# Expert blocks and first norm: bounds read at two loop ends, one 4 MB weight transfer per expert, another order of experts, and no barrier behind the first norm

## The reference, cut to what matters

```
h  = rms_norm(x, g)  * (1 + scale)  + shift        # 1024 tokens
hc = rms_norm(xc, g) * (1 + cscale) + cshift       # 256 tokens
u  = h @ w_in ; uc = hc @ w_in                     # gated convolution, attention, ...
```

```
hid = silu(x_block @ w_gate[e]) * (x_block @ w_up[e])      # 512 wide
y   = hid @ w_down[e]                                      # 1024 wide
out[token] += weight * y[row of the token]                 # two rows for each token
```

## Time and profile before

| what | us |
|---|---|
| median of three runs | 4255.51 |
| the profiled execution | 4245.79 |
| its span | 4243.7 |
| PE busy, in the span | 3750.0 |
| DVE busy | 1724.6 |
| ACT busy | 975.1 |
| expert stage of the first layer, first matmul to last store started | 2473 to 3031 |
| expert stage of the second layer, likewise | 3613 to 4164 |

### The profile page before, as it was taken

The page is one execution under the profiler, slowest core; times in us unless marked ns, Lnnn a source line. Parts: engine busy times, 40 slices in busy tenths (PEclk is TensorE's granted clock), DMA queues, the critical chain, the costliest instruction groups (busy, mean ns, idle before and its releaser), DMA issues.

```text
span 4243.7 us, 81332 instructions
## 1 busy us (share of the span) xinstructions
PE 3750.0 (88%) x29964; PEld 2095.4 (49%) x29965; DVE 1724.6 (41%) x3835; ACT 975.1 (23%) x2286; POOL 272.6 (6%) x453
## 2 busy tenths in 40 slices
PE   5997888999999889999988969989499998899874
PEld 3564665555444555444565445555344444455443
DVE  2585666413202664152465334434331114343335
ACT  3003545302001332131053212222120002222211
POOL 0000000000000000000000021111100000211111
PEclk9998999999999999999999989999799998999997
DMA  8111222101101000110142178999511113799994
GB/s 314 44 40 40 100 88 113 70 24 40 59 20 40 1 1 11 50 48 31 60 160 102 75 283 354 425 426 425 221 40 40 40 61 120 318 366 418 426 426 150
DMA packets 94333, 644.11 MB, mean 152 GB/s; under 512 B 18640, under 2 KB 41240, under 8 KB 60752
## 3 DMA queue, kind: packets, MB, share of 16 engines
q10 hardware_dynamic: 28896, 386.28, 21.5%
q1 hardware_dynamic: 46928, 194.98, 12.4%
q0 software_dynamic: 18336, 60.44, 4.1%
HBM read 594.70 MB, written 46.92 MB: 151 GB/s over the span
## 4 chain that ended last, share of the span: by engine, by line
PE 37%; DMA 13%; DVE 4%; issue 3%; SPq 2%; ACT 1%; DVEq 1%; ACTq 1%; POOLq 0%; POOL 0%
PE banks L258 23%; DMA y_tok<-arena 7%; PE banks L2407 7%; DMA arena<-in_w_gu 4%; SPq L2360 2%; PE banks L2416 2%; DMA arena<-y_tok,arena 1%; PE banks L1519 1%; DVE arena L1634 1%; PE banks L2122 1%; PE banks L2402 1%; PE banks L467 1%; DMA h_tok<-arena 0%; PE banks L2398 0%; ACTq L2300 0%
## 5 line engine op out<-in xcount | busy, mean ns | idle before, releaser
L258 PE MATMUL banks<-arena 128*128 128x512 f32 (+2 forms) x4544 | 1750.0, 547 | 39.0 <-ACTq L137 16.9
L258 PEld LDWEIGHTS banks<-arena 128*128 128x128 f32 x4544 | 841.4, 191 | 935.6 <-issue 884.6
L2407 PE MATMUL banks<-arena 128*32 128x256 f32 x10240 | 611.1, 387 | 48.2 <-DMA arena<-in_w_gu 41.1
L2407 PEld LDWEIGHTS banks<-arena 128*32 128x32 f32 x10240 | 324.4, 111 | 278.9 <-issue 104.8
L2416 PE MATMUL banks<-arena 128*32 128x256 f32 x5120 | 302.5, 384 | 65.4 <-DVE arena L2561 40.9
L2416 PEld LDWEIGHTS banks<-arena 128*32 128x32 f32 x5120 | 167.8, 110 | 194.0 <-DVE arena L2561 94.3
L1588 PE MATMUL banks<-arena 128*64 128x128 f32 x1952 | 161.8, 285 | 54.9 <-ACT arena L1601 39.2
L945 DVE SCALAR_TENSOR_TENSOR arena<-arena 128x1024 f32<-128x1024 f32 x240 | 195.9, 879 | 0.2 <-DVEq L137 0.2
L301 DVE SCALAR_TENSOR_TENSOR arena<-banks,arena 128x512 f32<-128x512 f32 (+1 forms) x72 | 51.9, 721 | 333.3 <-PE banks L258 333.3
L2373 POOL DMA_INDIRECT arena<-h_tok,arena x176 | 172.1, 978 | 142.2 <-POOL arena L2370 141.4
L1519 PE MATMUL banks<-arena 64*128 64x256 f32 (+2 forms) x768 | 130.1, 470 | 37.7 <-ACT arena L1690 32.8
(11 more groups left out here) (327 smaller groups left out, 3500.8 us busy)
## 6 DMA issues: line engine op xcount, KB each, us to landing
arena<-in_w_gu ACTq DMA_DIRECT2D x120, 2048.0 KB, 16.6
arena<-in_w_dn ACTq DMA_DIRECT2D x60, 2048.0 KB, 17.2
arena<-in_w_ada SPq DMA_DIRECT2D x24, 2048.0 KB, 7.3
y_tok<-arena SPq DMA_DIRECT2D x648, 32.0 KB
arena<-in_w_gu SPq DMA_DIRECT2D x8, 2048.0 KB, 10.8
y_tok<-arena POOLq DMA_DIRECT2D x1, 12800.0 KB, 36.3
arena<-in_ab_w_ada SPq DMA_DIRECT2D x6, 2048.0 KB, 9.5
arena<-in_cd_w_ada SPq DMA_DIRECT2D x6, 2048.0 KB, 7.3
```

The costliest lines, as they stand in the source:

```text
L258: last = pe.matmul(self.bank_of(g, n), lhsT, rhs, start=k == 0, stop=k == KT - 1)
L2407: last = pe.matmul(bank(2 + j)[32 * q:32 * q + 32, 0:256], xbT[:, 128 * j + 32 * q2:128 * j + 32 * q2 + 32], w_gu[slot][j][:, 4 * q2 + q], ...
```

## The change

It does five things. (1) The loop bounds are read one at each loop end, no longer two at every other. (2) The gate and up weights of an expert are one transfer, with one semaphore, of 128 rows of 32 KB. (3) The barrier `ab_norm` goes; ACT adds to `nrm_h` after each scaled tile and PE waits for that (L249 to L251, which are there already); POOL's small clears move ahead of `ab_mod`, its large one and the clearing transfer wait for the last tile of the divide. A buffer moves for that. (4) In the order of experts the one with the second smallest key (the fewest blocks but for expert 31) goes to the last position, and the others behind the middle move up by two. (5) Four small DVE operations are added in the routing for that.

```
-        M_AB = Mods(("ab",), STAGE)
+        M_AB = Mods(("ab",), STAGE + 10240)
...
                         a.activation(h_of[w_][:, k, t0:t0 + n], h_of[w_][:, k, t0:t0 + n], ACT.Identity,
-                                     scale=self.scale(k, w_), bias=self.shift(k, w_))
+                                     scale=self.scale(k, w_), bias=self.shift(k, w_)).then_inc(nrm_h, 1)
+
+            def made(self, rows, k):
+                i = 2 if rows[1] is h_c else rows[2] // 512
+                return KT * i + k + 1
...
-                self.wa, self.wb, self.wd = ([s(f"{w_}_slot{j}") for j in range(2)]
-                                             for w_ in ("w_half_a", "w_half_b", "w_down"))
+                self.wg, self.wd = ([s(f"{w_}_slot{j}") for j in range(2)] for w_ in ("w_gate_up", "w_down"))
...
+                link(d.tensor_scalar(last, place, float(E - 2), float(E - 1), ALU.is_equal, ALU.mult))
+                link(d.tensor_scalar(head, place, float(E - 1), 2.0, ALU.is_equal, ALU.mult))
                 link(d.tensor_scalar(place, place, 2.0, 1.0, ALU.mult, ALU.add))
-                link(d.tensor_scalar(mirror, place, -1.0, 2.0 * E - 1.0, ALU.mult, ALU.add))
+                link(d.tensor_scalar(mirror, place, -1.0, 2.0 * E - 3.0, ALU.mult, ALU.add))
                 link(d.tensor_tensor(place, place, mirror, ALU.min))
+                link(d.tensor_tensor(place, place, last, ALU.add))
+                link(d.tensor_tensor(place, place, head, ALU.add))
...
-            def load_gu(self, eng, slot, e, part):
-                eng.dma_start(mem(SLOTS[slot] + UNIT * part, UNIT),
-                              t["w_gu"][self.l, bass.ds(e, 1), :, UNIT * part:UNIT * part + UNIT].rearrange(
-                                  "e p n -> p (e n)")).then_inc((self.wa, self.wb)[part][slot], 16)
+            def load_gu(self, eng, slot, e):
+                eng.dma_start(mem(SLOTS[slot], 2 * UNIT), t["w_gu"][self.l, bass.ds(e, 1)].rearrange("e p n -> p (e n)")
+                              ).then_inc(self.wg[slot], 16)
...
                     c0, c1, c2 = bring()
-                    c3, c4 = first(2 * p + 1, 1, c1, c2, p, lambda: [self.cum(eng, 2 * p + 3), self.cum(eng, 2 * p + 4)])
+                    c3 = first(2 * p + 1, 1, c1, c2, p, lambda: self.cum(eng, 2 * p + 3))
                     second(2 * p, 0, c0, c1, p)
-                    first(2 * p + 2, 0, c2, c3, p + 1)
+                    c4 = first(2 * p + 2, 0, c2, c3, p + 1, lambda: self.cum(eng, 2 * p + 4))
                     second(2 * p + 1, 1, c1, c2, p)
                     carry((c2, c3, c4))
...
-                    pe.wait_ge(self.wa[slot], 16 * nth + 16)
-                    pe.sem_inc(passed, 1)
-                    pe.wait_ge(self.wb[slot], 16 * nth + 16)
+                    pe.wait_ge(self.wg[slot], 16 * nth + 16)
                     pe.sem_inc(passed, 1)
...
-                        for part in range(2):
-                            self.load_gu(a, slot, e, part)
+                        self.load_gu(a, slot, e)
...
-            close("ab_norm")
-            P_AB_A.pe(pe)
+            P_AB_A.pe(pe, N_AB)
...
-            close("ab_mod")
             for ct in range(4):
                 for a0, n in ((0, HALF), (HALF + S, 2 * HALF), (S + L + 3 * HALF, HALF)):
                     g.memset(G_U[:, ct, a0:a0 + n], 0.0)
-            close("ab_norm")
-
+            close("ab_mod")
+            g.wait_ge(nrm_x, nrm_total[0])
             g.memset(zeros, 0.0).then_inc(pool_done, 1)
```

More of the change, by code:

```diff
@@ L536, in mod_dve @@
             M_AB.finish(d, link)
-        nrm_sq, nrm_mm, nrm_rt, nrm_x, nrm_rc = (sem(s_) for s_ in ("nrm_sq", "nrm_mm", "nrm_rt", "nrm_x", "nrm_rc"))
+        nrm_sq, nrm_mm, nrm_rt, nrm_x, nrm_rc, nrm_h = (
+            sem(s_) for s_ in ("nrm_sq", "nrm_mm", "nrm_rt", "nrm_x", "nrm_rc", "nrm_h"))
         nrm_total = [0, 0]
@@ L583, in act @@
                         a.activation(h_of[w_][:, k, t0:t0 + n], h_of[w_][:, k, t0:t0 + n], ACT.Identity,
-                                     scale=self.scale(k, w_), bias=self.shift(k, w_))
+                                     scale=self.scale(k, w_), bias=self.shift(k, w_)).then_inc(nrm_h, 1)
+            def made(self, rows, k):
+                i = 2 if rows[1] is h_c else rows[2] // 512
+                return KT * i + k + 1
         N_AB = Norm(True, lambda k, w_: gs["ab"][:, k, w_:w_ + 1], lambda k, w_: mod["ab"][:, k, w_:w_ + 1])
-        nrm_h, nrm_add, nrm_rd = sem("nrm_h"), sem("nrm_add"), sem("nrm_rd")
-        flow = dict(sq=nrm_total[0], mm=nrm_total[1], rt=nrm_total[1], rc=nrm_total[1], x=nrm_total[0], h=0, add=0,
+        nrm_add, nrm_rd = sem("nrm_add"), sem("nrm_rd")
+        flow = dict(sq=nrm_total[0], mm=nrm_total[1], rt=nrm_total[1], rc=nrm_total[1], x=nrm_total[0], h=nrm_total[0], add=0,
                     rd=0)
@@ L2020, in program @@
         mirror = mem(M0 + 4226, 33, n=32)
+        last, head = (mem(M0 + 4324 + 33 * i, 33, n=32) for i in range(2))
         above = mem(M0 + 4259, 32, n=32)
@@ L2331, in in_turn @@
                 c0, c1, c2 = bring()
-                c3, c4 = first(E - 3, 1, c1, c2, None, lambda: [self.cum(eng, E - 1), self.cum(eng, E)])
+                c3 = first(E - 3, 1, c1, c2, None, lambda: self.cum(eng, E - 1))
                 second(E - 4, 0, c0, c1)
-                first(E - 2, 0, c2, c3)
+                c4 = first(E - 2, 0, c2, c3, None, lambda: self.cum(eng, E))
                 second(E - 3, 1, c1, c2)
@@ L2341, in blocks_sp @@
                 sp.wait_ge(stage_end, closed(("ev_attn", "od_conv")[self.l]))
-                for part in range(2):
-                    self.load_gu(sp, 1, 0, part)
+                self.load_gu(sp, 1, 0)
                 sp.wait_ge(stage_end, closed(("ev_out", "od_out")[self.l]))
-                for part in range(2):
-                    self.load_gu(sp, 0, E - 1, part)
+                self.load_gu(sp, 0, E - 1)
                 self.load_dn(sp, 0, E - 1)
@@ L2952, in _ @@
             close("m1_sum_final")
-STAGES = ["loads", "ab_mod", "ab_norm", "ab_gated", "ab_qkv", "ab_heads", "ab_attn", "ab_z",
+STAGES = ["loads", "ab_mod", "ab_gated", "ab_qkv", "ab_heads", "ab_attn", "ab_z",
           "ab_out_cd_f", "cd_four", "cd_qkv", "cd_attn", "cd_z", "cd_out_ev_in", "ev_attn",
```

## The result

The changed kernel took 4312.93 us (median of 3 runs, 4306.7 to 4315.09) against 4255.51, a ratio of 1.0134 (95% interval 1.0111 to 1.0157): 1.3% slower. The forecast was 4334, with a range of 4295 to 4375. The profiled execution took 4306.7 us with a span of 4304.5, 60.8 more than the span before.

The account below looks back on a forecast made before the run. Expert stages were taken as bound by the queue of y stores, slowed by streaming weights. Terms +45 +36 +4 +5 +1.7 -13 = +78.7 us on 4255.5 gave 4334 us; own range 4295 to 4375, 8-in-10 range 4232 to 4368.

Parts of the forecast that it names:

- The merge, +90 predicted: Expert stages: 32 KB rows double each turn beside gate and up loads, so stores of y fall behind; +90 us.
- full-queue stretches: Later part of each expert stage, stores always queued: 1.6 blocks a pair left out, 3.9 us a pair; +45 and +36 us.
- early stretches: Earlier part of each expert stage, store queue short at times: SP's waits take back half the loss; +4 and +5 us.
- The spacing of 10 us: Sign in stretches of full DMA share: SP's blocks 10 us apart on average if turns double, 7 if not.
- groups of rows: DMA engines in expert stages: if turns go by whole packets of 9 to 17 descriptors, the merge changes no turn.
- The first rival: Expert stages: turns don't lengthen, stores stay at 7 us a block; 4240 us, chance 0.32.
- The second, a third of the term: Expert stages: turns lengthen by less, a third of the +90, so +30; 4274 us, chance 0.11.
- The saving of up to 120 us: 60 merged gate and up transfers, 2 us fixed cost each by the skill page; taken as already covered.
- The norm, -13: First norm: PE's first product starts at 63.3 us, not 76.16, then waits for weights; -13 us, bounds -11 and -15.
- Routing, bounds, one start less: Four DVE operations in routing +1.7 us; bounds at loop ends 0 (-8 to +8); one ACT transfer start less 0 (0 to -5).
- The order, 0: End of expert stages: a shorter last down loop is hidden behind the queue of stores; 0, bounds 0 and -16 us.
- The third rival: End of expert stages: PE's tail sets the end, so the order brings some -7 and -9 us; 4224 us, chance 0.05.

Follow-up runs that it names:

- two_transfers_16k: The changed kernel with each expert's gate and up weights again as two transfers of 128 rows of 16 KB: 4237.62 us, 0.9969 of the kernel before.

## Why the prediction was right, and where not

**The merge, +90 predicted.** The mechanism was right and the size a little off: the stages grew by 39.8 and 36.2, together 76, for 49 and 41, and the merge alone cost 74. The term that was too large is the one for the full-queue stretches, +45 and +36. As SP starts blocks there, the pace went from 6.96 to 7.37 us in layer 1 and from 7.07 to 7.61 in layer 2, which is 1.9 and 2.5 us for the 4.7 blocks of a pair of experts, not the 3.9 of the sum: over 11.5 and 9.3 pairs some 22 and 24 us. The rest had come before and came behind. By the stage's own clock (from the first gate and up matmul) the 17th block of stores was started 10.2 us later than before the change in layer 1 (at 159 us for 149) and 4.0 in layer 2, although DVE's y of that block was 3 us earlier in both; the 71st was 35.1 and 49.7 late, the last 39.9 and 36.2. So the +4 and +5 for the early stretches weren't too large. These delays swing by 10 to 20 us from block to block, as 20 and 8 us take turns, so the split is rough.

**The spacing of 10 us was wrong.** I wrote that SP would need 10 us a block on average. It started 51 blocks in 376 us, 7.4 us each, against 54 and 6.96:

```profile
L2366 SPq ALU_OP  x51: 12/33/37, 2627.8 to 2995.5; - x51
...
L2366 SPq ALU_OP  x46: 3/33/37, 3843.3 to 4183.3; - x46
```

By my own sum the average should have been (32.6 + 3.9)/4.7 = 7.8: 10 us is the pace beside a stream without gaps, and I had myself argued that gaps must come. What gave way was the weights: in the same 340 us 128.0 MB moved instead of 144.0, and 16 MB at 423 GB/s are 38 us. The wrong sign would have told me I was wrong ("if SP's blocks keep their 7 us") while I wasn't. The right sign was the alternation of 20 and 8 us and DVE's waits.

**The turn.** The Trainium skill says in DMA: Bandwidth & Descriptors (section Queues, rings and completion order) that an engine drains a whole packet, typically 9 to 17 descriptors, before it turns to another queue. The trace doesn't agree. From 2640 to 2980 before the change (queue: packets, MB, share), weights, stores and gathers:

```profile
q10 hardware_dynamic: 8966, 130.63, 90.2%
q1 hardware_dynamic: 9264, 6.33, 5.7%
q0 software_dynamic: 2544, 6.95, 5.2%
```

That is one packet of stores for one of weights. The trace also keeps each packet with its queue, size, start and length, though not its engine. I put each packet behind the one that ends where it starts (they join within a few ns), which gives 16 sequences. In them the weight packets stand alone between packets of other queues in 8,313 of 8,555 cases before, and in 4,828 of 4,993 after; where two ends coincide the engine is a guess, and with such ties drawn at random it is still 9 in 10. A typical piece is 1 KB, 16 KB, 1 KB, 16 KB, signal, 16 KB. A packet of 16 KB takes 0.611 us in the median, one of 32 KB 1.213, so the large rows move at the same rate and only the turn is longer. A weights' signal (4 bytes, 9 ns) takes a turn of its own.

The prediction said that by groups of rows the merge would change no turn. That doesn't follow: a group of eight rows of 32 KB would be twice as long as one of eight rows of 16 KB. So the run times alone don't rule groups out; the order of the packets does. The first rival (turns don't lengthen) would have needed 4240; it fell. The second, a third of the term, fell as well: 76 of 90. The saving of up to 120 us that the prediction set beside its sum isn't there either: with equal rows one transfer for two lost 10.7 us. And a gather of x is not 9 packets an engine, as the prediction has it, but 3: the third line has 48 packets for each of 53 gathers, four rows of 1 KB in one packet. Only the sum's upper bound used it.

**The norm, -13.** The start of the first product fell by 13.4 us, for the cause named (weights late next, 3.52 us of waiting). By the time of the kernel alone it is -10.6, and -13 lies inside the interval. That a shorter pause spares the lower clock was left open, and the trace says no: the granted clock was at its lower level (0.50) from 62.4 to 65.9, PE's first 3.1 us, and before from 62.8 to 79.9, so for PE's first 3.7 us. The stretch ends 13.7 us sooner, hardly more than it starts. The other 2.3 of the 16.0 lie in dense work that the change doesn't touch, and here the profile was lucky: in the eleven other kernels with this norm the first gate and up matmul came at 2462.2 to 2469.5, so 3.6 to 10.9 us sooner than before, not 16.0.

**Routing, bounds, one start less.** +1.7, 0 and 0. None can be told from nothing here; the last goes with the 10.7 us that one transfer of 16 KB rows loses to two, so if anything it has the other sign.

**The order, 0.** No gain is seen, for the reason given: SP's last 11 blocks come 2.8 us apart both times, and the last of them starts 12.4 us behind DVE's end before and 15.9 after. The third rival's mechanism is real: where no queue stands, the order was worth 12.4 us (some 14 without its four operations), against the 7 and 9 I had given it (16 for both).

**The sum.** In the profiles: -16.0 + 39.8 + 0.3 + 36.2 + 0.4 = +60.7, for +78.7 predicted. The stages are 14 of the difference, the start 4, and of the start's -16.0 some 5 us or more are luck, as above. The parts run by themselves add up to about the same: +74.4 for the merge and -11.5 for all the rest (`two_transfers_16k`) are +62.9; the medians give +57.4.

## What to carry to other kernels

Where a large stream and a small one share the DMA engines, the length of the large one's rows sets how fast the small one goes: in these traces each small packet waits for one large row. Count packets on the page to learn what a row is, and choose the length by which stream has slack; here 8 KB freed the stores and cost 1% of the rate, 4 KB cost 4% of it, and 32 KB cost the kernel 1.7% of its time. When a chain names a queue of stores behind the last sum, don't expect to see what shortens the tail ahead of it until that queue is gone: the order of experts was worth 12.4 us without the queue and showed no gain with it.

## What the hardware did that I had not expected

Transfers into 64 neighbouring partitions took 2.47 us for a packet of 32 KB and brought the stream to 241 GB/s with the engines 0.94 busy; into every other partition, with the same rows and bytes, a packet took 1.21 us and the stream moved 384. At a full share the rate fell with the row's length, 423, 419, 407 GB/s at 16, 8 and 4 KB. And with one transfer of 256 rows for each expert the kernel was 10.7 us slower than with two of 128; a signal packet does take a turn of its own, but whether the missing ones are the cause stays open, since the number of transfers and of packets changed together.
